# Layer norms behind the down projections: tiles centred as they come, with the mean of the first two

## What is computed

```python
def layer_norm(x, g, b):
    xc = xf - jnp.mean(xf, -1, keepdims=True)
    var = jnp.mean(xc * xc, -1, keepdims=True)
    return xc * lax.rsqrt(var + LN_EPS) * g + b
...
f = swiglu(h, ffn_w_gate, ffn_w_up, ffn_w_down)     # (silu(h @ wg) * (h @ wu)) @ wd
h = layer_norm(DEEPNORM_ALPHA * h + 0.5 * f, ln_g, ln_b)
```

## Time and profile before

| | us |
|---|---|
| median of 3 runs | 1542.81 |
| lowest and highest run | 1537.6, 1543.05 |
| profiled execution, its own time | 1535.55 |
| span of that execution in the profile | 1533.7 |
| PE busy | 1429.0 (93%) |
| DVE busy | 866.7 (57%) |
| ACT busy | 627.0 (41%) |
| POOL busy | 383.5 (25%) |

### The profile page before, as it was taken

One profiled execution on the slowest core, in us unless ns is written; L12 is line 12 of the kernel. 1 busy time (PEld: TensorE's weight loads), 2 busy tenths in 40 slices (PEclk: granted clock), 3 DMA queues, 4 the chain that ended last, 5 costly groups with the idle time before them and its releaser, 6 DMA issues.

```text
span 1533.7 us, 30765 instructions
## 1 busy us (share of the span) xinstructions
PE 1429.0 (93%) x12062; PEld 1349.7 (88%) x12062; DVE 866.7 (57%) x1179; ACT 627.0 (41%) x938; POOL 383.5 (25%) x405
## 2 busy tenths in 40 slices
PE   7999999877998799999999999979997879999997
PEld 7999999766698589999999999969887749999996
DVE  4444446975363366555465554468777556655544
ACT  4333336522142343333353333265573434433323
POOL 3333001442130222115101115000007652111330
PEclk9999999999799799999999999999998989999999
DMA  7545533300052044455434455424333024454541
GB/s 281 167 163 180 169 122 107 102 2 30 32 192 84 30 170 165 164 163 185 152 108 164 163 169 181 145 76 132 127 121 138 30 89 146 138 164 163 188 156 46
DMA packets 50617, 203.30 MB, mean 133 GB/s; under 512 B 5697, under 2 KB 5697, under 8 KB 49761
## 3 DMA queue, kind: packets, MB, share of 16 engines
q1 hardware_dynamic: 46224, 181.03, 35.7%
q0 software_dynamic: 4016, 19.81, 3.5%
q10 hardware_dynamic: 288, 1.18, 0.2%
HBM read 192.17 MB, written 9.83 MB: 132 GB/s over the span
## 4 chain that ended last, share of the span: by engine, by line
PE 80%; DVE 10%; ACT 5%; issue 4%; POOL 1%; DMA 0%; DVEq 0%; ACTq 0%; POOLq 0%
PE gemm L2403 22%; PE gemm L2407 22%; PE gemm L2404 21%; ACT whi L2353 2%; DVE wlo L2358 2%; PE gemm L2428 1%; PE job L2444 1%; DVE M L1947 1%; PE gemm L504 1%; PE job L2410 1%; PE job L1605 1%; PE job L1528 1%; PE job L697 1%; PE job L1631 1%; PE job L728 0%
## 5 line engine op out<-in xcount | busy, mean ns | idle before, releaser
L2403 PE MATMUL gemm<-xhi,whi 128*128 128x290 f32 (+1 forms) x2040 | 623.8, 306 | 31.0 <-DVE wlo L2358 20.5
L2358 DVE TENSOR_TENSOR wlo<-raw,whi 128x1024 fp32r<-128x1024 f32 (+1 forms) x319 | 426.1, 1336 | 354.7 <-ACT whi L2353 354.5
L2353 ACT ACTIVATE whi<-raw 128x1024 fp32r<-128x1024 f32 (+1 forms) x319 | 358.5, 1124 | 631.5 <-PE gemm L2407 628.1
L2407 PE MATMUL gemm<-xlo,whi 128*128 128x290 f32 (+1 forms) x2040 | 612.7, 300 | 4.2 <-DVE xlo L391 4.1
L2404 PE MATMUL gemm<-xhi,wlo 128*128 128x290 f32 (+1 forms) x2040 | 610.0, 299 | 0.0
L2403 PEld LDWEIGHTS gemm<-xhi,whi 128*128 128x128 f32 x2040 | 391.5, 192 | 48.3 <-DVE wlo L2358 23.2
L2407 PEld LDWEIGHTS gemm<-xlo,whi 128*128 128x128 f32 x2040 | 390.4, 191 | 5.8 <-DVE xlo L391 4.8
L2404 PEld LDWEIGHTS gemm<-xhi,wlo 128*128 128x128 f32 x2040 | 391.4, 192 | 2.5
L2403 PE MATMUL gemm<-hhi,whi 128*128 128x288 f32 x704 | 208.9, 297 | 2.1 <-POOL hlo L2767 1.8
L2407 PE MATMUL gemm<-hlo,whi 128*128 128x288 f32 x704 | 209.6, 298 | 0.0
L2404 PE MATMUL gemm<-hhi,wlo 128*128 128x288 f32 x704 | 208.5, 296 | 0.0
(11 more groups left out here) (403 smaller groups left out, 1414.2 us busy)
## 6 DMA issues: line engine op xcount, KB each, us to landing
raw<-in_w_dram SPq DMA_DIRECT2D x255, 512.0 KB, 3.5
raw<-in_w_dram SPq DMA_DIRECT2D x64, 704.0 KB, 4.0
M<-in_ret_in_dram POOLq DMA_DIRECT2D x1, 2048.0 KB, 9.3
out_ret_s_dram<-M POOLq DMA_DIRECT2D x1, 2048.0 KB, 8.1
...
```

Source lines behind the costliest of these rows:

```text
L2353: nc.scalar.activation(whi[c % SPL][:, 0:w], raw[c % RAW][:, 0:w], ACT.Copy).then_inc(hi_ready, 1)
L2358: nc.vector.tensor_tensor(wlo[c % SPL][:, 0:w], raw[c % RAW][:, 0:w], whi[c % SPL][:, 0:w].bitcast(F32), ALU.subtract).then_inc(lo_ready, 1)
L2403: pe.matmul(bank[:, 0:w_], whi[s][:, w], hi[:, f0 + q, 0:w_], start=first, stop=False)
L2407: mm = pe.matmul(bank[:, 0:w_], whi[s][:, w], lo[:, f0 + q, 0:w_], start=False, stop=last)
```

## The change

The norms behind the down stages (0, 2, 3, 5) are computed otherwise; norms 1 and 4 stay as they were.

- Behind down unit 4 PE multiplies tiles 0 and 1 with the 1/1024 matrix (a new job, `first`); ACT copies the result times 4 into `first_mean`: the mean over those two tiles.
- DVE subtracts `first_mean` from each tile right after its residual (`centre`; the first three tiles together behind unit 5). ACT squares the tile two units later (`tile_parts`), POOL adds up both the tiles (xsum) and their squares (in x[0]).
- Behind the stage PE needs two matmuls for the rest of the mean (`rest`: xsum and the last tile) and two for the squares (`spread`). ACT reads the rest of the mean twice, as it is and squared (`rest_parts`); DVE subtracts the squared rest from the sum of squares (`deviation`), ACT takes the root, DVE the reciprocal.
- In norms 0, 3 and 5 the rest of the mean is subtracted from the tiles, by DVE from tiles 0 to 2 (`take_rest`) and by POOL from tiles 3 to 7. The unused matmuls behind norms 0 and 3 are 13 in place of 16.
- In norm 2 (`BOTH`) the rest is not subtracted from the tiles. xhi and xlo are made in the down stage already; the second extra column carries minus the gain, and DVE adds rest times that column to each result of the up stage (a second operation for each unit, `gate_moved`, `up_moved`). `rest` and `spread` stand inside the first up unit, at its last input tile; the unused matmuls behind norm 2 are gone. POOL's `late_x` gets one more operation for each tile.
- The down stages are listed unit by unit.

```diff
+WRITTEN_OUT = ("za", "zb", "abo", "down")
 WARM = 16
...
+EARLY = {0: 0, 2: 1, 3: 2, 5: 3}
+BOTH = 2
...
+                        if first_unit and late == BOTH and q == DT - 1:
+                            rest(late)
...
+            def first_tiles(n):
+                def behind(u):
+                    if u == 4:
+                        if n == 0:
+                            pe.wait_ge(sem("const_in"), 64)
+                        use = TABLE[NORM_STAGE[n]][3]
+                        bank = start(("first", n))
+                        for d in range(2):
+                            pe.wait_ge(bank_free[2 * d], use[2 * d] + 1)
+                        pe.matmul(bank[:, 0:T], C("mean"), r3[:, 0, :], start=True, stop=False)
+                        pe.matmul(bank[:, 0:T], C("mean"), r3[:, 1, :], start=False, stop=True
+                                  ).then_inc(filled[bank_of(("first", n))], 1)
+                return behind
+
+            def rest(n):
+                bank = start(("mean", n))
+                pe.wait_ge(sem("summed"), n + 1)
+                pe.matmul(bank[:, 0:T], C("mean"), xsum[:], start=True, stop=False)
+                pe.wait_ge(sem("early"), DT * EARLY[n] + DT)
+                pe.matmul(bank[:, 0:T], C("mean"), r3[:, DT - 1, :], start=False, stop=True
+                          ).then_inc(filled[bank_of(("mean", n))], 1)
+
+            def spread(n):
+                bank = start(("var", n))
+                pe.wait_ge(sem("squares_summed"), (DT - 2) * (EARLY[n] + 1))
+                pe.matmul(bank[:, 0:T], C("mean"), x[:, 0, :], start=True, stop=False)
+                pe.wait_ge(sem("early_sq"), DT * EARLY[n] + DT)
+                pe.matmul(bank[:, 0:T], C("mean"), x[:, DT - 1, :], start=False, stop=True
+                          ).then_inc(filled[bank_of(("var", n))], 1)
+
             def norm(n):
-                pe.wait_ge(sem("const_in"), 64)
+                if n == BOTH:
+                    return
+                if n in EARLY:
+                    rest(n)
+                    spread(n)
+                    keep_warm(n, 13)
+                    return
                 bank = start(("mean", n))
...
                     if j % 2 == 0:
-                        act.wait_ge(bank_free[j], i + (use[j] + 1))
+                        if LATE_OF[k + 1] == BOTH:
+                            act.wait_ge(sem("gate_moved"), i * 2 + (j // 2 + 1))
+                        else:
...
+            def operand_edges(n):
+                nc.scalar.activation(xhi_all[:, :, T:T + 1], par[:, LN_B + DT * n:LN_B + DT * n + DT].unsqueeze(2), ACT.Copy)
+                nc.scalar.activation(xhi_all[:, :, T + 1:TX], par[:, LN_G + DT * n:LN_G + DT * n + DT].unsqueeze(2), ACT.Copy,
+                                     scale=-1.0).then_inc(sem("bias_hi"), 1)
+
+            def tile_parts(n, d):
+                act.wait_ge(sem("early"), DT * EARLY[n] + d + 1)
+                if n == BOTH:
+                    nc.scalar.activation(xhi[:, d, :], r3[:, d, :], ACT.Copy, scale=pc("ln_g", n * DT + d)
+                                         ).then_inc(x_hi, 1)
+                if d < DT - 1 or n != BOTH:
+                    tile_square(n, d)
+
+            def tile_square(n, d):
+                nc.scalar.activation(x[:, d, :], r3[:, d, :], ACT.Square).then_inc(sem("early_sq"), 1)
+
+            def early_tiles(n):
+                def consume(i, j, u0, use):
+                    u = 4 * i + j
+                    if u == 1 and n == BOTH:
+                        operand_edges(n)
+                    elif u == 5:
+                        if n == 0:
+                            act.wait_ge(sem("const_in"), 64)
+                        key = ("first", n)
+                        act.wait_ge(*full(key))
+                        nc.scalar.activation(first_mean[:], jobb[bank_of(key)][:, 0:T], ACT.Copy, scale=4.0
+                                             ).then_inc(drained[bank_of(key)], 1)
+                    elif u == 7:
+                        for d in range(3):
+                            tile_parts(n, d)
+                    elif u > 7 and u % 2 == 1:
+                        tile_parts(n, (u - 3) // 2)
+                return consume
+
+            def rest_parts(n):
+                key = ("mean", n)
+                act.wait_ge(*full(key))
+                src = jobb[bank_of(key)][:, 0:T]
+                nc.scalar.activation(rest_mean[:], src, ACT.Copy).then_inc(sem("rest"), 1)
+                nc.scalar.activation(first_mean[:], src, ACT.Square).then_inc(drained[bank_of(key)], 1)
+
+            def root(n):
+                act.wait_ge(*out(("var", n)))
+                eps = C("eps")[:, 1:2]
+                nc.scalar.activation(rstd[:, 0:T], rstd[:, 0:T], ACT.Sqrt, bias=eps).then_inc(sem("root"), 1)
+
...
-                if n == 0:
-                    act.wait_ge(sem("const_in"), 64)
                 preload(ACT.Sqrt)
-                late = n in LATE_SCALE
-                if late:
+                if n == BOTH:
+                    tile_parts(n, DT - 1)
                     split_hi(act, 0, second_unit(n), width(second_unit(n)))
-                    nc.scalar.activation(xhi_all[:, :, T:TX], bc(par[:, LN_B + DT * n:LN_B + DT * n + DT], 2, 2), ACT.Copy
-                                         ).then_inc(sem("bias_hi"), 1)
+                    tile_square(n, DT - 1)
+                    rest_parts(n)
+                    u = second_unit(n) + 1
+                    split_hi(act, 0, u, width(u))
+                    root(n)
+                    return
+                if n in EARLY:
+                    tile_parts(n, DT - 1)
+                    rest_parts(n)
+                    root(n)
+                    if second_unit(n):
+                        split_hi(act, 0, second_unit(n), width(second_unit(n)))
+                    finish_norm(n)
+                    return
...
@@ -2624,12 +2724,25 @@
                     if j % 2 == 0:
                         wait_count(dve, sem("hidden"), i * 2 + (FT * k + h - 1))
                         V.tensor_tensor(sg[:, h, :], gemm[j][:, 0:TX], rstd[:], ALU.mult).then_inc(bank_free[j], 1)
+                        if both:
+                            dve.wait_ge(bank_free[j], i + (use[j] + 1))
+                            V.scalar_tensor_tensor(out=sg[:, h, 0:T], in0=rest_mean[:], scalar=sg[:, h, T + 1:TX],
+                                                   in1=sg[:, h, 0:T], op0=ALU.mult, op1=ALU.add
+                                                   ).then_inc(sem("gate_moved"), 1)
                     else:
                         V.tensor_tensor(ub[:, h, :], gemm[j][:, 0:TX], rstd[:], ALU.mult).then_inc(bank_free[j], 1)
+                        if both:
+                            dve.wait_ge(bank_free[j], i + (use[j] + 1))
+                            V.scalar_tensor_tensor(out=ub[:, h, 0:T], in0=rest_mean[:], scalar=ub[:, h, T + 1:TX],
+                                                   in1=ub[:, h, 0:T], op0=ALU.mult, op1=ALU.add
+                                                   ).then_inc(sem("up_moved"), 1)
                     if not isinstance(i, int) or i or j:
                         split_lo(dve, i, u0 + j + 2, next_width(u0, kind, i, j))
                     if j % 2 == 1:
-                        dve.wait_ge(bank_free[j], i + (use[j] + 1))
+                        if both:
+                            dve.wait_ge(sem("up_moved"), i * 2 + (h + 1))
+                        else:
+                            dve.wait_ge(bank_free[j], i + (use[j] + 1))
                         dve.wait_ge(sem("gate_on"), i * 2 + (FT * k + h + 1))
                         wait_count(dve, hid_lo, i * 2 + (FT * (k + 1) + h - 1))
                         V.scalar_tensor_tensor(out=hb[:, h, :], in0=ub[:, h, 0:T], scalar=ub[:, h, T:T + 1],
...
+            def centre(n, d, use):
+                if d == 2:
+                    dve.wait_ge(*out(("first", n)))
+                for t in ((0, 1, 2) if d == 2 else (d,)):
+                    dve.wait_ge(bank_free[2 * (t % 2)], use[2 * (t % 2)] + t // 2 + 1)
+                    nc.vector.tensor_tensor(r3[:, t, :], r3[:, t, :], first_mean[:], ALU.subtract
+                                            ).then_inc(sem("early"), 1)
+                if n == BOTH and d > 2:
+                    for t in ((0, 1, 2) if d == 3 else (d - 1,)):
+                        unscaled_low(n, t)
+
+            def residual(scale, kind, late=None, early=None):
                 def consume(i, j, u0, use):
                     if kind == "down":
                         if j % 2 == 0:
...
                 return consume
...
+            def deviation(n):
+                dve.wait_ge(*full(("var", n)))
+                dve.wait_ge(*out(("mean", n)))
+                nc.vector.tensor_tensor(rstd[:, 0:T], jobb[bank_of(("var", n))][:, 0:T], first_mean[:], ALU.subtract
```

(80 more changed lines are left out.)

100 lines of the change are left out of this document (49 added, 51 removed).

## The result

The changed kernel takes 1546.13 us (median of 7 runs) against 1538.47 us of the kernel before beside it: the ratio is 1.0046, 95% interval 1.0029 to 1.0063. It is slower, by about 7 us; the forecast was 1542.5 us and no difference. The forecast stood on 1542.81, the median of three runs of the kernel before, and the seven runs beside the changed kernel have their median 4.3 us lower; so that 1542.5 lies only 3.6 us from the measured time is no merit of the sum. What missed is the change: -0.3 us forecast, +7 measured. The profiled execution took 1548.99 us, with a span of 1547.0, where that of the kernel before had 1533.7.

The account below looks back on a forecast made before the run. PE was taken to bound the kernel, with 80% of the span on its chain. Norms 0, 2, 3 and 5 summed as -1.1 + 2.2 + 0 - 1.4 = -0.3 us against 1542.81, giving 1542.5; range 1535.5 to 1548.5.

Parts of the forecast that it names:

- 1.07 us earlier than before: Norms 0 and 3: the reciprocal starts 1.07 us earlier, of 3.3 us that the shorter chain offers.
- -2.1 and -1.07: Norms 0 and 3: gains before adding 1.0 us each for the new matmuls, giving -1.1 and 0.
- Rival B: Behind norms 0 and 3: PE's clock also falls after some 2.7 us without work; +1.1 in all, 1543.9; chance 0.18.
- the bound of 2.3: Norm 0, first unit behind it: a slow-clock stretch would cost up to 2.3 us; 1.4 was taken.
- Norm 2: PE idle 4.3 us, then half clock costing 1.5 (bounds 0 and 2.3); with 0.7 for the norm, +2.2.
- 0.2 once or twice: Down stages, units 5 and 7, where three tiles come together: if they overrun, 0.2 us once or twice.
- Norm 5: Reciprocal 2.4 us earlier, with one wait behind POOL (bounds -3.0 and -2.0); with +1.0 for the matmuls, -1.4.
- The down stages: Each of four: two new matmuls cost 1.0 us of PE, exposed; centring and unit-by-unit listing cost nothing.
- 0 to 1.4: Each down stage: listing unit by unit may make PE wait for instructions, 0 to 1.4 us; taken as nothing.
- C: Norm 2's up stage: POOL's split delays DVE, the weight split comes 0.45 late; +9.6 in all, 1552.4; chance 0.10.
- A: Behind norm 2: PE's clock holds; -1.8 in all, 1541.0; chance 0.15.
- D: Split ahead of the reciprocal costs nothing: norms 0 and 3 gain 2.2 more each, norm 5 3.0; -5.3, 1537.5; chance 0.12.

Follow-up runs that it names:

- experiment 8: Changed kernel with POOL subtracting the rest of the mean from one column of each of its five tiles instead of 288; ratio 1.0008 to the kernel before.
- Experiment 1: Changed kernel with 21 unused matmuls in place of 13 behind norms 0 and 3, and 8 behind norm 2; ratio 1.0021 to the kernel before.
- first trace: The changed kernel's first profiled execution, nothing edited; it took 1548.99 us, span 1547.0.
- experiment 6: Changed kernel with the two matmuls of the first tiles' mean run twice in each down stage; ratio 1.0065 to the kernel before.
- experiment 3: Changed kernel with the second unit's split, in norms 0 and 3, before ACT's last square and in DVE's wait for the mean; ratio 1.0018 to the kernel before.
- second trace: The changed kernel profiled once more, nothing edited; stages and norms sum to +6.5 us, and its span excess over the kernel before's first trace is 8.7 us.

## Why the prediction was wrong

**The step that failed** is the reciprocal of norms 0 and 3, "1.07 us earlier than before". The prediction counted ACT's split and DVE's split as all that stands in its way, and weighed POOL's subtractions against `take_rest` in norm 5 only. In norms 0 and 3 the same five instructions run beside `take_rest` and beside the split. From the first `take_rest` to the reciprocal it took 4.66 us (226.24 to 230.90), where experiment 8 has 3.58 (224.98 to 228.56): 1.08 us, as much as the whole gain that was forecast, and the reciprocal came only 0.2 us earlier than in the kernel before (6.54 and 6.53 behind the residual's end, for 6.71 and 6.77). Experiment 8 shows the rest too: with POOL's part cut, the two norms come out at -2.24 and -1.33, where the prediction had -2.1 and -1.07, and the kernel is level with the one before. That its sum, too, is about the forecast's -0.3 is chance: there the stages cost 6.0 where 4.0 was taken, and norm 5 gains 3.35 where 2.4 was.

The Trainium skill's page "SBUF — State Buffer", section "Who interferes with whom", says that a DVE instruction with two SBUF inputs contends with a GpSimd instruction that reads SBUF, and one with at most one such input, outside the two-port modes, doesn't. The rows here agree: `take_rest` 1.06 for 0.46, the split 1.77 for 1.23, the scaling 4.76 for 3.52; but `deviation`, which reads one of its inputs from PSUM, took 0.44 and the reciprocal 1.94 beside a running POOL. The prediction quoted that rule, and applied it to one norm out of three.

**Rival B came on top**, which had 0.18; the forecast's sum had nothing for it. PE had 1.17 and 2.30 us without work around two products, and the clock fell behind norm 0, as it did behind norm 3 after 1.16 and 2.75. The prediction's number for it was 1.4 in norm 0 and nothing in norm 3, because ACT would cover it. Experiment 1 gives 2.1 us and 0.8 against the first trace, 1.3 and nothing against the second; the bound of 2.3 held. At full clock, in experiment 1, the two marks still stand 0.95 and 1.31 us behind the forecast (16.49 for 17.64 - 2.1, 18.27 for 18.03 - 1.07): this is the conflict's own part. That the conflict also brought the clock down is not shown in general: without it the clock held behind norm 0 and fell behind norm 3, one trace each, after 2.28 and 2.27 us without work, where rival B had 2.7.

**Norm 2** was right in its mechanism: 4.3 us without work (4.24), then the half clock (0.52, for 3.45 us), norm +1.2 (+0.65 and +1.65). Its reciprocal was to come 1.3 us nearer to the residual; it came 0.4 nearer in the first trace and 0.6 farther in the second, where the half clock lasted longer. Its stage cost 2.07 to 2.24 where 1.0 was taken. Of the rest 0.64 is one stop, where DVE's split is late behind the unit in which three tiles and their low parts come together; the prediction had put "0.2 once or twice" there.

**Norm 5** came out at -1.99, at the weaker of its two bounds, -3.0 and -2.0; -2.4, for one wait behind POOL, was taken.

**The down stages** are a second term that was too small: 6.45 us for four, where 4.0 was taken. The two matmuls are right, 0.97 against 1.0, shown by experiment 6. The 0.4 a stage beyond it is the slower pace of the products and not the wait for instructions for which the prediction had 0 to 1.4; that it lies inside those bounds is luck.

**Rivals.** C didn't come: the up stage behind norm 2 shows no waits of PE for the split, and the difference to the kernel before neither grows nor shrinks in it. A fell with the window of norm 2. D's condition was made true by experiment 3, and its gain came in part: norm 3's reciprocal starts 1.74 us earlier than in the changed kernel and its mark stands 2.6 us earlier than in the first trace, 1.7 than in the second, where D has 2.2. Against the kernel before the mark gained 1.5 and not D's 3.3, as `take_rest` was still held (1.06).

By terms: -0.3 forecast, +7 measured; norms 0 and 3 account for +3.1 + 2.1 of the 7.5 by the first trace, the stages for +2.45, norm 5 for +0.4, norm 2 for -0.5. By the second trace norms 0 and 3 account for +2.3 + 1.3 and norm 2 for +0.45.
